# Recurrent-gate products of a hybrid decoder layer: four full-array products per pass against eight 64x64 quadrant products in two places

## The reference: what is computed

```python
xb = x32.reshape(B, T, N_RG_BLOCKS, RG_BLOCK)
r = sigmoid(einsum('btnc,ncd->btnd', xb, w_r).reshape(B, T, D_RNN) + b_r)
i = sigmoid(einsum('btnc,ncd->btnd', xb, w_i).reshape(B, T, D_RNN) + b_i)
log_a = -RG_C * r * softplus(-lam)
a = exp(log_a)
b = sqrt(-expm1(2.0 * log_a)) * (i * x32)
h_t = a_t * h_(t-1) + b_t
```

## Time and profile before

| | |
|---|---|
| time, median of 3 runs | 808.5 us (806.24 to 808.62) |
| profiled execution: its own time | 807.31 us |
| its span, first to last instruction | 805.5 us |
| TensorE clock granted, mean | 0.987 of full |
| PE busy | 777.1 us, 96% of the span |
| DVE busy | 472.3 us, 59% |
| ACT busy | 358.1 us, 44% |
| POOL busy | 62.4 us, 8% |
| share of the last-ending chain that is PE | 91% |
| the gates' products (line 1004), share of that chain | 0.9% |

### The profile page before, as it was taken

One profiled execution on the slowest core, in us unless ns is written; L12 is line 12 of the kernel. 1 busy time (PEld: TensorE's weight loads), 2 busy tenths in 40 slices (PEclk: granted clock), 3 DMA queues, 4 the chain that ended last, 5 costly groups with the idle time before them and its releaser, 6 DMA issues.

```text
span 805.5 us, 16337 instructions
## 1 busy us (share of the span) xinstructions
PE 777.1 (96%) x6019; PEld 736.3 (91%) x6019; DVE 472.3 (59%) x739; ACT 358.1 (44%) x614; POOL 62.4 (8%) x142
## 2 busy tenths in 40 slices
PE   3999999999999999999999899999999999999996
PEld 2879998999898899996889899999999999999996
DVE  5556646636646643675558877777777776222223
ACT  6235534534534541333465455555555565222222
POOL 3321102011010110004000000000000010000000
PEclk9899999999999999999999999999999999999998
DMA  6654335335422122635443233333333224323222
GB/s 205 176 165 134 101 117 142 91 97 146 126 75 83 52 80 72 218 105 167 148 132 104 56 101 105 104 104 104 104 103 96 61 96 135 99 72 91 78 65 111
DMA packets 148746, 89.09 MB, mean 111 GB/s; under 512 B 8594, under 2 KB 142186, under 8 KB 148715
## 3 DMA queue, kind: packets, MB, share of 16 engines
q1 hardware_dynamic: 146014, 81.63, 34.4%
q0 software_dynamic: 2384, 6.40, 2.3%
q10 hardware_dynamic: 316, 0.66, 0.3%
HBM read 81.85 MB, written 6.81 MB: 110 GB/s over the span
## 4 chain that ended last, share of the span: by engine, by line
PE 91%; DVE 1%; ACT 1%; issue 1%; DVEq 0%; ACTq 0%
PE ps L843 32%; PE ps L1158 25%; PE ps L1223 17%; PE ps L1057 6%; PE ps L1127 3%; PE ps L932 1%; PE ps L945 1%; PE ps L962 1%; PE ps L1004 1%; PE ps L907 1%; PE ps L918 1%; PE ps L975 1%; PE ps L1065 0%; PE ps L1092 0%; PE ps L991 0%
## 5 line engine op out<-in xcount | busy, mean ns | idle before, releaser
L1762 DVE TENSOR_TENSOR w_lo<-w_raw,w_hi 128x1024 fp32r<-128x1024 f32 (+1 forms) x68 | 80.9, 1191 | 141.5 <-ACT w_hi L1300 141.2
L1300 ACT ACTIVATE w_hi<-w_raw 128x1024 fp32r<-128x1024 f32 (+1 forms) x68 | 70.0, 1031 | 142.2 <-PE ps L1223 82.6
L843 PE MATMUL ps<-xin_hi,w_hi 128*128 128x272 f32 x576 | 126.9, 302 | 0.0
L843 PE MATMUL ps<-xin_hi,w_lo 128*128 128x272 f32 x576 | 119.5, 289 | 0.0
L843 PE MATMUL ps<-xin_lo,w_hi 128*128 128x272 f32 x576 | 119.4, 289 | 0.0
L843 PEld LDWEIGHTS ps<-xin_hi,w_hi 128*128 128x128 f32 x576 | 90.6, 190 | 8.9 <-issue 7.6
L843 PEld LDWEIGHTS ps<-xin_lo,w_hi 128*128 128x128 f32 x576 | 91.0, 189 | 0.0
L843 PEld LDWEIGHTS ps<-xin_hi,w_lo 128*128 128x128 f32 x576 | 90.6, 190 | 0.0
L1223 PE MATMUL ps<-hid_hi,w_hi 128*128 128x272 f32 x352 | 76.0, 291 | 0.4 <-DVE hid_lo L2140 0.4
L1223 PE MATMUL ps<-hid_lo,w_hi 128*128 128x272 f32 x352 | 75.0, 287 | 0.0
L1223 PE MATMUL ps<-hid_hi,w_lo 128*128 128x272 f32 x352 | 74.9, 288 | 0.0
(11 more groups left out here) (335 smaller groups left out, 1753.5 us busy)
## 6 DMA issues: line engine op xcount, KB each, us to landing
w_raw<-in_w_in_dram SPq DMA_DIRECT2D x72, 256.0 KB, 3.2
g_raw<-in_w_gate_up_dram SPq DMA_DIRECT2D x40, 256.0 KB, 3.9
w_raw<-in_w_down_dram SPq DMA_DIRECT2D x40, 256.0 KB, 2.9
u_raw<-in_w_gate_up_dram SPq DMA_DIRECT2D x20, 256.0 KB, 3.0
e_raw<-in_w_gate_up_dram SPq DMA_DIRECT2D x20, 256.0 KB, 4.4
kc<-in_cache_k_dram SPq DMA_DIRECT2D x64, 64.0 KB, 1.9
vc<-in_cache_v_dram SPq DMA_DIRECT2D x64, 64.0 KB, 2.0
wo_raw<-in_w_out_dram SPq DMA_DIRECT2D x12, 256.0 KB, 4.0
```

The costliest lines, as they stand in the source:

```text
L843: mm = e.matmul(ps[:, bank + h, 0:HT], wt[:, kw, :], xt[:, kx, h * HT:h * HT + HT], start=first and wt is wh and xt is xh, stop=last and ( ...
L1300: e.activation((to or w_hi[s])[:, 0:k, :], w_raw[s][:, 0:k, :], ACT.Copy).then_inc(hi_done, count)
L1762: e.tensor_tensor(wl[:, 0:k, :], w_raw[s][:, 0:k, :], wh[:, 0:k, :].bitcast(F32), ALU.subtract).then_inc(lo_done, count)
```

## The change

The four `rg` places of a pass become two, `rg_gates(0)` and `rg_gates(1)`, both in tile 6. Each makes both gates of one token half in four products of 64x64, one for every pairing of the upper or lower 64 rows with the upper or lower 64 output partitions: gate r straight (block 0 to partitions 0 to 63, block 1 to 64 to 127) into `M_BANK`, gate i crossed over (block 0 to partitions 64 to 127, block 1 to 0 to 63) into `S_BANK`. For that second bank `rg_gates(0)` also waits for `logits_done` (the DVE has read the last scores), and the sample scores of the next pass wait for `mi_free`. ACT reads a half in three Tanh instead of two, the crossed gate with 64 rows at a time, which puts the blocks back in order; the crossed bias is loaded in two pieces instead of one. The second Tanh now follows both halves of both gates. `M_BANK`'s uses drop from 9 to 7 to a pass, and all counts with them.

```diff
-            for src, r0, n in ((conv_w, 0, 16), (conv_b, 16, 4), (rg_b_r, 20, 4), (rg_b_i, 24, 4),
+            for src, r0, n in ((conv_w, 0, 16), (conv_b, 16, 4), (rg_b_r, 20, 4),
                                (rg_lambda, 28, 4), (norm_mix_post, 32, 8), (norm_ffn_pre, 40, 8), (norm_ffn_post, 48, 8)):
                 e.dma_start(prow[r0:r0 + n, :], AP(src.tensor, 0, [[P, n], [1, P]])).then_inc(par_in, 16)
+            for blk in range(2):
+                e.dma_start(prow[24:28, RGB * blk:RGB * blk + RGB], AP(rg_b_i.tensor, RGB * (1 - blk), [[P, 4], [1, RGB]])
+                            ).then_inc(par_in, 16)
...
@@ def scores_s
                     e.wait_ge(tile_free[1], it * 4 + 2)
+                    e.wait_ge(mi_free, it * 7 + 1)
...
-                def rg(g, h):
-                    if g == 0 and h == 0:
+                def rg_gates(h):
+
+                    if h == 0:
                         e.wait_ge(conv_step, it * 8 + 8)
                         e.wait_ge(bd_in, it * 64 + 64)
-                    mi_wait(5 + 2 * g + h)
-                    e.matmul(ps[:, M_BANK, 0:EH], bd[:, g, :], xc[:, EH * h:EH * h + EH], start=True,
-                             stop=True).then_inc(mi_ready, 1)
+                        e.wait_ge(logits_done, it * 9 + 10)
+                    count = e.to_reg(it * 7 + (6 + h))
+                    e.wait_ge(consts, 2)
+                    e.wait_ge(mi_free, count)
+                    for g, bank in enumerate((M_BANK, S_BANK)):
+                        for blk in range(2):
+                            rows = slice(RGB * blk, RGB * blk + RGB)
+                            out = RGB * (blk ^ g)
+                            mm = e.matmul(ps[out:out + RGB, bank, 0:EH], bd[rows, g, rows], xc[rows, EH * h:EH * h + EH],
+                                          start=True, stop=True)
+                    mm.then_inc(mi_ready, 1)
...
-                rg(0, 0); part(5, 3, 5); rg(0, 1); probs_T(4); scores(0); part(5, 5, 8)
-                begin(6); rg(1, 0); part(6, 0, 3); rg(1, 1); probs_T(5); part(6, 3, 8)
+                part(5, 3, 5); probs_T(4); scores(0); part(5, 5, 8)
+                begin(6); rg_gates(0); part(6, 0, 3); rg_gates(1); probs_T(5); part(6, 3, 8)
...
-                def rg_gate(use, dst):
-
-                    g, h = divmod(use - 5, 2)
-                    e.wait_ge(mi_ready, it * 9 + (use + 1))
-                    e.activation(dst[:, EH * h:EH * h + EH], ps[:, M_BANK, 0:EH], ACT.Tanh, bias=prm_it[:, 5 + g:6 + g],
-                                 scale=0.5).then_inc(mi_free, 1)
+                def rg_half(h):
+
+                    cols = slice(EH * h, EH * h + EH)
+                    e.wait_ge(mi_ready, it * 7 + (h + 6))
+                    e.activation(th[:, cols], ps[:, M_BANK, 0:EH], ACT.Tanh, bias=prm_it[:, 5:6], scale=0.5)
+                    for blk in range(2):
+                        src = slice(RGB * (1 - blk), RGB * (1 - blk) + RGB)
+                        last = e.activation(ti[RGB * blk:RGB * blk + RGB, cols], ps[src, S_BANK, 0:EH], ACT.Tanh,
+                                            bias=prm_it[src, 6:7], scale=0.5)
+                    last.then_inc(mi_free, 1)
...
-                rg_gate(5, th)
-                rg_gate(6, th)
                 probs_copy(4); exp(0, 0); exp(0, 1)
 
                 next_hi(6)
                 gate(5)
-                rg_gate(7, ti)
-
+                rg_half(0)
+                rg_half(1)
+                e.wait_ge(mi_free, it * 7 + 8)
                 e.activation(th[:, :], th[:, :], ACT.Tanh, bias=prm_it[:, 7:8], scale=prm_it[:, 7:8]).then_inc(th_done, 1)
-                rg_gate(8, ti)
                 probs_copy(5)
```

More of the change, by code:

```diff
@@ L579, in iteration @@
                         e.dma_start(biasT[:, :, :], src).then_inc(bias_in, 16)
-                        e.wait_ge(mi_free, it * 9 + 1)
+                        e.wait_ge(mi_free, it * 7 + 1)
                         for g, wrg in enumerate((rg_w_r, rg_w_i)):
@@ L592, in iteration @@
                         load_pages(cache_k, kc, kc_in, it + 1, j - 5)
-                e.wait_ge(mi_free, it * 9 + 4)
+                e.wait_ge(mi_free, it * 7 + 4)
                 for g, (op, os) in enumerate(((new_k_prompt, new_k_sample), (new_v_prompt, new_v_sample))):
@@ L600, in iteration @@
                 if not last:
-                    e.wait_ge(mi_ready, it * 9 + 4)
+                    e.wait_ge(mi_ready, it * 7 + 4)
                     load_pages(cache_v, vc, vc_in, it + 1, 0)
@@ L870, in _ @@
                 x_T(tt)
-            e.wait_ge(par_in, 160)
+            e.wait_ge(par_in, 176)
             e.transpose(ps[:, 2, 0:56], prow[:, :], ident[0:56, 0:56]).then_inc(small_T, 1)
@@ L898, in mi_wait @@
                 def mi_wait(use):
-                    e.wait_ge(mi_free, it * 9 + (use + 1))
+                    e.wait_ge(mi_free, it * 7 + (use + 1))
                 def cache_T(f):
@@ L1027, in _ @@
                     e.wait_ge(st_saved, PAIRS)
-                    e.wait_ge(mi_free, 9 * PAIRS + 1)
+                    e.wait_ge(mi_free, 7 * PAIRS + 1)
                     for f in range(PAIRS):
@@ L1403, in _ @@
                 probs_copy(1); exp(2, 0); exp(2, 1)
-                e.wait_ge(mi_ready, it * 9 + 3)
+                e.wait_ge(mi_ready, it * 7 + 3)
                 e.activation(tok[:, 0, 0:TT, :], ps[:, M_BANK, :].rearrange("p (tt c) -> p tt c", c=P), ACT.Copy
                              ).then_inc(mi_free, 1)
-                e.wait_ge(mi_ready, it * 9 + 4)
+                e.wait_ge(mi_ready, it * 7 + 4)
                 e.activation(o_s[:, :], ps[:, M_BANK, 0:NJ * P], ACT.Copy).then_inc(mi_free, 1)
@@ L1413, in _ @@
                 e.activation(halves(gb[:, :]), two(0), ACT.Copy).then_inc(tile_free[0], 1)
-                e.wait_ge(mi_ready, it * 9 + 5)
+                e.wait_ge(mi_ready, it * 7 + 5)
                 for h in range(2):
@@ L1886, in _ @@
                 scale(3, 0); scale(3, 1)
-                e.wait_ge(mi_ready, it * 9 + 1)
+                e.wait_ge(mi_ready, it * 7 + 1)
                 e.wait_ge(kv_out, it * 64 + 64)
                 e.tensor_copy(tok[:, 1, 0:TT, :], ps[:, M_BANK, :].rearrange("p (tt c) -> p tt c", c=P)).then_inc(mi_free, 1)
-                e.wait_ge(mi_ready, it * 9 + 2)
+                e.wait_ge(mi_ready, it * 7 + 2)
                 e.tensor_copy(tok[0:TS, :, TT, :], ps[0:TS, M_BANK, 0:2 * P].rearrange("p (g c) -> p g c", g=2)
```

## The result

| | before | changed |
|---|---|---|
| time, median | 807.24 us (805.97 to 808.62, 14 runs) | 809.76 us (808.88 to 811.07, 14 runs) |
| ratio of the times, 95% | | 1.0032 (1.0024 to 1.0040) |
| profiled execution, own time | 807.31 us | 810.02 us |
| its span | 805.5 us | 808.2 us |

What follows compares the result with a forecast made beforehand. PE was taken to bound the kernel, through its own time and waits before it. Four passes of +0.63 us in tile 6, nothing back from tile 5, made +2.5, put at +2.6: 808.5 + 2.6 = 811.1 us, range 808.2 to 813.5.

Steps and rivals of the forecast that it cites:

- What bounds the kernel: Whole span: PE, busy 96%, sets the time through its own work and the waits put in front of it.
- what a gate product costs: Old gate places on PE: 0.47 us each, following steps at normal pace; four make 1.88 us a pass.
- What a quadrant place costs: Tile 6: 0.80 and 0.77 us for the two places against 0.94 replaced, +0.63 us a pass (0.60 to 0.76).
- What tile 5 gives back: Before probs_T(4): the 0.94 us removed becomes PE waiting for DVE's second division; gain 0, at most 0.15 us.
- ACT and the bank: Ahead of rg_gates(1): ACT's three reads, 0.37 us apart, clear the bank 0.3 us before PE wants it; no wait.
- The longer road to the recurrence: After the gates: DVE starts 3.0 us later, covered before the next pass with some 0.5 us left; cost 0.
- Small edits: Extra Tanh reads and ACT self-wait already counted; extra bias load, mi_free wait and bd reload cost 0.
- Sum: Four passes of 0.63 us give +2.5 us, put at +2.6; profiled execution 809.9 us, median 811.1 us.
- Tile 5 gives its time back: Rival at probs_T(4): PE keeps all 0.94 us a pass, -1.2 us in all, 807.3 us; chance 0.12.
- this rival together with cheap places: Tile 5 keeps its 0.94 us and split shapes add no fixed cost: -3.6 us, 804.9 us; chance 0.05.
- Cheap places: Rival in tile 6: no shape cost, a place takes 0.48 us; +0.1 us in all, 808.6 us; chance 0.10.
- The quadrants take turns on a bank: Rival in tile 6: row halves sharing a bank exclude each other, 1.72 us a place; +10 us, 818.5; chance 0.08.

Runs made afterwards that it cites:

- experiment 2: Kernel before, with one wait added so POOL's second gelu product starts after DVE's second division of tile 5: 807.48 us, ratio 0.9998.
- experiment 5: Kernel before, its four places kept, the second half of each gate made as two diagonal 64x64 products: 810.12 us, ratio 1.0036.
- experiment 7: Changed kernel with rg_gates(1) one contraction step later in tile 6: pass 65.68 us, kernel 810.29 us, ratio 1.0042.
- experiment 6: Changed kernel with all eight quadrant products in one place behind tile 6's third step: 808.06 us; with POOL's product also held behind DVE's division: 805.12 us.
- experiment 1: Changed kernel with one wait added so POOL's second gelu product starts after DVE's second division of tile 5: 806.85 us, ratio 0.9989.
- experiment 3: Changed kernel with probs_T(4) and scores(0) one contraction step later in tile 5: 807.08 us, ratio 0.9993.
- experiment 4: Changed kernel's two places, each with two full-array products instead of four quadrants, gate i not crossed: 811.04 us, ratio 1.0040.
- experiment 8: Kernel before with diagonal 64x64 second gate halves, tile 5's moved directly ahead of scores(0), and POOL's product held behind DVE's division: 809.48 us, ratio 1.0035.

## Why the prediction was right, and where it was off

**What bounds the kernel; what a gate product costs.** Both held. Single full products measure 0.46 to 0.47 us in experiments 2 and 5, and every change of a pass below came out as a sum on PE's path.

**What a quadrant place costs.** 0.80 us was said of the first and 0.82 is measured; 0.77 of the second, and 0.78 is measured where it doesn't wait (0.63 + 0.37 - 0.22, experiment 7). The price of the shape, 0.31 to 0.35 us, lies in the range taken from `scores`, `values` and `values_s`. The starts of the records show where the first place's 0.35 us is: 0.09 us more than usual between the last matmul and the first record of the place, 283 ns between its two groups of records where the two of a full product are 233 ns apart, and the second matmul behind it starts another 0.22 us later than behind a full product. Only the first group of a place is 50 ns late: in experiment 6 the later ones follow at 232 and 233 ns, so that this part looks like the first stationary load, which nothing covers. The Trainium skill's span formula ("TensorE: Matmul & The Clock Gate", Part 3), by which tile 6 would have grown by 0.02 us, leaves all of it out.

**What tile 5 gives back.** Gain 0 was said, with 0.15 at most; 0.04 us is measured. The reason holds too: experiments 1 and 3 give back 0.86 and 0.75 us by taking away the wait for `scaled`, and experiment 2 shows that the gain of experiment 1 isn't the POOL wait's own. The sign that it rested on, a weight load at 138.80, 0.13 us behind DVE's end, is there in the changed kernel too: its chain has 0.12 us of issue between DVE's end at 139.27 and 139.39. The idle time came out at 0.7 us in the view of waits, not 0.8 to 0.9, since `probs_T(4)`'s four transposes now stand with 0.65 us (0.44 before): the exposed load is counted as theirs.

**ACT and the bank.** This step failed. "That clears by 0.3 us: no wait"; the runs show 0.13 us of wait in every pass. The reads were taken at 0.37 us from one to the next. ACT's timeline of the changed kernel has them at 0.49:

```profile
144.44 0.48 ACT L1395 ACTIVATE th<-ps,prm_it 128x276 f32<-128x276 f32 x1
144.93 0.98 ACT L1398 ACTIVATE ti<-ps,prm_it 64x276 f32<-64x276 f32 x2
...
148.33 0.85 ACT L1443 ACTIVATE th<-th,prm_it 128x552 f32<-128x552 f32 x1
```

Three reads end at 144.93 + 0.98 = 145.91, which is T + 2.98 (T, the end of tile 5, is 142.93 here), where the prediction had T + 2.72. The 0.37 of the earlier trace rows was the distance from a Tanh that reads PSUM to one that reads SBUF. But two reads of 128 rows from PSUM follow each other as fast, in the kernel of experiment 4:

```profile
145.17 0.48 ACT L1391 ACTIVATE th<-ps,prm_it 128x276 f32<-128x276 f32 x1
145.54 0.49 ACT L1392 ACTIVATE ti<-ps,prm_it 128x276 f32<-128x276 f32 x1
```

There the second starts 0.1 us before the first ends. Around a crossed read of 64 rows this overlap is missing, and such a read takes as long as one of 128. So the term that was mis-sized is the step between reads, 0.49 for 0.37, and it came with reading gate i in crossed halves; whether the 64 rows, the crossing or the start at row 64 takes the overlap away, no run here separates. PE comes to the place at 146.00, 0.09 us behind the reads' end, and that is too close. The timeline of PE's weight loads, changed kernel:

```profile
142.86 0.21 PEld L1016 LDWEIGHTS ps<-xc,bd 64*64 64x64 f32 x8
...
146.03 0.24 PEld L1016 LDWEIGHTS ps<-xc,bd 64*64 64x64 f32 x8 [0.25 <-issue]
```

The first place's loads start 0.07 us ahead of its turn in the chain (142.93), the second's 0.03 us behind theirs (146.00), which is 0.12 us behind ACT's end, the same distance as at `probs_T(4)` behind DVE's. Put at nothing, the wait measured 0.13 us a pass: 0.5 us over four passes, a fifth of the result.

**The longer road to the recurrence.** "DVE starts 3.0 us later" was half a microsecond short, and it was covered as said. DVE's timeline:

```profile
149.22 0.45 DVE L1945 TENSOR_SCALAR dd<-th 128x552 f32<-128x552 f32 x1 [3.93 <-ACT th L1443]
153.92 1.23 DVE L1777 TENSOR_TENSOR w_lo<-w_raw,w_hi 128x1024 fp32r<-128x1024 f32 x1
...
162.14 0.73 DVE L1975 TENSOR_TENSOR ocat_lo<-dd,ocat_hi 128x544 f32 x1 [1.22 <-ACT ocat_hi L1456]
```

It starts 4.12 us later than the 145.10 of the earlier trace rows; 0.58 us of it is that this part of the pass itself is later (142.93 against 142.35), and 3.5 us is the longer road. Of the half microsecond that was missing, 0.2 us is that ACT gets the second half's products later (146.81, T + 3.88, where the prediction had T + 3.65), and 0.3 us is the reads' pace again. The `w_lo` moved to 153.92 and ends at 155.15, when PE has worked for 2 us on tile 7. ACT's read of the recurrence's end starts at

```profile
161.32 0.65 ACT L1456 ACTIVATE ocat_hi<-dd 128x544 f32 x1
```

and so 1.36 us later than in the earlier trace rows, exactly as much as `values` is later (150.88 against the 149.52 of the earlier trace rows): against PE's work it has not moved at all. No new wait of PE appears at the next pass.

**Small edits.** Cost 0, as said: no row of PE's waits names `prow`, `bd` or `logits_done`.

**Sum.** +2.6 us was said (2.5 from the terms and 0.1 by hand, for which no row stood), +2.5 us is measured. That they agree so well is luck in part: a pass grew by 0.75 us where the terms said 0.63 (the bank's wait 0.13, the two places 0.03, tile 5's turn -0.04), 3.0 us over four passes, while the medians differ by 2.5 and the spans by 2.7. The profiled time was put at 809.9 and came at 810.02; the absolute median, 811.1, is 1.3 us too high, because the 808.5 of three runs shown lay 1.3 us above the 807.24 of fourteen.

**The rivals.** *Tile 5 gives its time back*: not so here, but experiment 1 is that case made real: 4 x (64.94 - 65.05) = -0.4 us by its passes, -0.9 us by its ratio. It falls short of the rival's -1.2 us, for the most part since the bank's wait stays (0.5 us). The sum for this rival together with cheap places takes 0.04 us where the prediction's own figure for tile 6 is 0.02: -3.7 us, not -3.6. *Cheap places*: excluded by every place above. *The quadrants take turns on a bank*: excluded, where the partitions differ. The eight records of a place, some 0.23 us of streaming each, fit into 0.62 us; the four first ones start 0, 7, 13 and 20 ns after each other, the four second ones 283 ns behind, although upper and lower rows write the same bank.

## What to carry to other kernels

Packing small products onto parts of the array costs a fixed sum per place in the program (here 0.3 us, among full products in float32), so count places, not products: two quadrants alone lost 0.3 us, four in a place gained 0.1, eight in one place gained 0.6. Before taking work out from in front of a consumer, look at what the consumer waits for: a load that starts 0.1 us behind another engine's end, instead of with the record before it, says that the work in front of it may be only cover, as it was here. Then shorten what releases it, here by one wait that keeps POOL off DVE's 0.35 us division, or move the consumer.

## What the hardware showed beyond what was expected

- **Quadrants share a bank.** Products of the upper and the lower 64 rows write the same PSUM bank, at different partitions, at the same time, with no turn taken: 0.62 us for eight records of 0.23 us of streaming each.
- **ACT's reads of PSUM do not shorten with fewer rows, and crossed halves lose the overlap.** 64x276 takes 0.49 us as 128x276 does. Two reads of 128 rows start 0.37 to 0.39 us apart (experiment 4), with a crossed read of 64 rows it is 0.49 us or a little more; with 552 columns each, a read takes 0.72 us and they are 0.75 us apart. A crossed output that must be read in two halves costs ACT a whole read more.
- **A price wherever the shape changes,** also from one split shape to another (experiment 8), and nearly the same for two quadrants as for four.
- **DVE's 128x256 division takes 0.35 us alone and 1.23 us when it starts 0.28 us after a POOL product of two inputs of 544 columns;** it then ends 0.15 us behind that product. A division begun 0.2 us before the product still takes 0.35 us. POOL's product takes 1.34 to 1.36 us in all cases: the delay is all on DVE's side.
